# Steps of an mLSTM and of a second attention moved by a slab inside one TensorE-bound program

## The chip, the cores and the metric

One core of a Trainium2 chip runs the whole program. The metric is device microseconds of one execution (us). Three runs of the kernel before gave 877.93, 878.43 and 878.40 us, median 878.4.

## The reference, cut to what matters

Two transformer blocks run one after the other on 256 tokens of width 1024. The change touches only the middle of the second: its mLSTM branch (4 heads of 128), its attention branch (8 heads of 64) and the first product behind them.

```python
# second block, z = h @ w_in_2 split into mq, mk, mv, mo, mi, mf, aq, ak, av, ga, gb
hm = mlstm_chunkwise(q, k, v, i, f)      # W = exp(D - m), SW = (q k^T) * W, h = SW v / max(|sum SW|, exp(-m))
hm = rms_norm_2(hm, m_norm_g)            # over the 128 of each head
ym = hm * sigmoid(mo)
ya = merge_heads(moba_attention(rope(aq), rope(ak), av))     # softmax attention, causal
merged = sigmoid(ga) * (ym @ p_mlstm) + sigmoid(gb) * (ya @ p_moba)
x = x + g1 * (merged @ w_out)
```

## The kernel before

All weights are one stream of 298 **slabs**, each 128 x 1024 floats. SyncE loads slab n + 7 when slab n is worked (line 545, tile raw, five buffers). A slab is split into two parts: ScalarE copies it to whi (`high_part`, line 2048, four buffers), VectorE subtracts to get wlo (`low_part`, line 1146). TensorE makes three products of 128 x 128 by 256 for each of the 8 weight blocks of a slab (lines 1101, 1103, 1104 in this part), 24 for a slab.

Everything else is cut into **steps**: generators that yield after each step. The table `STEPS` gives for each task three lists, for TensorE, VectorE and ScalarE; a number n says that this engine takes the task's next step behind slab n of its own program (208.5 is the middle of slab 209). No planner looks at times: the order on every engine is what the lists say, each engine runs its queue in order, and semaphores make a step wait for its inputs. Steps with the same number run in the order of the dictionary: "mlstm" ahead of "att2" ahead of "gates2".

- TensorE at number n: the steps come behind the last product of slab n.
- ScalarE at n: first `high_part(n + 4)`, which waits until TensorE has finished slab n, then the steps.
- VectorE at n: first `low_part(n + 3)`, then the steps. For n equal to `LATE` the split comes behind the steps (lines 2023 to 2028). But where a pair of output tiles ends with slab n, `low_part(n + 3)` has already been called at the head of the pair's event, ahead of the steps of n: `low_part` does a slab once only. In the product "gab" (slabs 200 to 215) this holds for each odd n, 215 among them, and not for 214.

The steps of the two mLSTM halves (two heads each; TensorE / VectorE / ScalarE) are: gate rows to all partitions (833); weights' maxima (1612 to 1626) and exponentials (2274); q k products (842, 843); weighting (1636 to 1659); transposes (850) and their copy (2282); output products "h" (857, 859); squares (2286, 2291) with hb and nlo (1666, 1671); sum of squares "n" (865, 866); root (2295); reciprocals (1676), gain (1681) and gate (1687); high part Ymhi (2301); low part Ymlo (1604, function `low`). The attention has four pairs of heads, each: scores "s" (879, 880), maxima (1385 to 1395), exponentials (2159), weighting (1401, 1406), transposes "t" (887), copy (2169), outputs "o" (899, 901), high part (2191, 2193), low part (1429). The task "gates2" turns four gate tiles by a sigmoid (2308), twice at its step 213.

The product "pm" begins with slab 216. It takes heads 0 and 1 of Ymhi and Ymlo in the first half of each output pair, heads 2 and 3 in the second half, so in the second half of slab 216 TensorE waits for the mLSTM's last output.

Of the kernel before, what the change touches and what calls it, by code (L numbers as in the profile page):

```python
# [158 lines left out]
def slab_ends():  # L159

    out, u = {}, 0
    for name, (kind, w, lead, c0, m, K) in zip(NAMES, plan()):
# [5 lines left out]
        else:  # L168
            u += m // 128 * K
            if u % SLAB == 0:  # L170
# [13 lines left out]

ROPE = (0, 2, 1, 3)

LATE = 214

BETWEEN = {40: 3, 68: 7, 183: 5}
STEPS = {  # L190
# [19 lines left out]
    "final": ([], [199, 205, 211, 215], []),  # L210
    "ifg": ([186, 188], [182, 185, 187, 189], [182, 183, 188]),
    "rope": ([], [189, 192, 195, 197], []),
    "mlstm": ([191, 193, 195, 197, 199, 203, 206, 208.5, 209.5, 211],
# [6 lines left out]
    "mfin": ([], [173, 175, 177, 178], [174, 176, 178, 179]),  # L220
    "mconv": ([], [*range(179, 188), 188, 188, 189], [182, 185, 188, 190]),
# [57 lines left out]
def build(nc, A, out):  # L279
# [16 lines left out]
    with ctx:  # L296
# [832 lines left out]
        def vector_program(v):  # L1129
# [4 lines left out]
            def low_part(s):  # L1134
                if s >= NS or s in lows:
                    return
                lows.add(s)
                w.wait_ge(*hi.at(s))
                if s >= NHL:
                    w.wait_ge(*mm.at("slab", s - NHL))  # L1140
                if name := beside(s):
                    x, y = narrow(name, s, raw[:, s % NRAW, :], joined[name][0])
                    v.tensor_tensor(narrow(name, s, raw[:, s % NRAW, :], joined[name][1])[1], x, y.bitcast(F32),
                                    ALU.subtract).then_inc(*lo_v.up(s))
                    return
                v.tensor_tensor(wlo[:, s % NHL, :], raw[:, s % NRAW, :], whi[:, s % NHL, :].bitcast(F32),  # L1146
                                ALU.subtract).then_inc(*lo_v.up(s))
# [868 lines left out]
            for name in NAMES:  # L2016
                for what, n in EVENTS[name]:
                    if what == "pair":
# [3 lines left out]
                        continue  # L2022
                    if n == int(n) and n >= 1 and n != LATE:
                        low_part(int(n) + 3)
                    for task in v_steps.get(n, ()):
                        if task in tasks:
                            next(tasks[task], None)
                    if n == LATE:
                        low_part(int(n) + 3)
# [696 lines left out]
```

## Time and profile before

| | us |
|---|---|
| median of three runs | 878.4 |
| profiled execution, its own time | 878.33 |
| its span, first to last instruction | 877.0 |
| TensorE busy | 867.4 (99%) |
| VectorE busy | 725.4 (83%) |
| ScalarE busy | 573.4 (65%) |
| granted TensorE clock, mean | 0.998 |

Busy time adds up the instructions of an engine. Matmuls overlap in the pipeline, so 99% says that TensorE is nearly always in work and not that it runs at its peak. The 1.33 us between the execution's time and its span lie around the program.

### The profile page before, as it was taken

The numbers are of one execution on the slowest core, as the hardware profiler recorded it, in microseconds if no ns is written. First come the engines' busy times: TensorE is split into PE (matmuls) and PEld (weight loads), VectorE is DVE, ScalarE is ACT, GpSimd is POOL, SyncE is SP. The second block draws the span as 40 slices with busy tenths as digits, with TensorE's granted clock in tenths as the row PEclk, the third lists the DMA queues.
The fourth block names the chain that finished last, engine by engine and source line by source line (L and its number), as shares of the span: only waits on it lengthen the run. The fifth ranks groups of instructions, "written<-read, shape, count | busy, mean of one in ns | idle before, by whom it ended". The sixth has DMA issues, their size and how long they took to land.

```text
span 877.0 us, 18438 instructions
## 1 busy us (share of the span) xinstructions
PE 867.4 (99%) x7308; PEld 846.6 (97%) x7308; DVE 725.4 (83%) x1168; ACT 573.4 (65%) x851; POOL 2.2 (0%) x10
## 2 busy tenths in 40 slices
PE   9999999999999999999999999999999999999996
PEld 7999989999999999999999999899999999999996
DVE  6788999899988899888887999989788985555554
ACT  7858466675696787664446879677786664444542
POOL 0000000000000000000000000000000000000000
PEclk9999999999999999999999999999999999999999
DMA  8866456566775789989895566754455566666551
GB/s 316 284 197 225 149 164 194 170 191 211 271 243 191 257 290 332 324 299 339 328 336 180 168 220 209 209 166 141 152 166 176 187 201 200 192 194 195 182 161 49
DMA packets 59045, 189.87 MB, mean 216 GB/s; under 512 B 8640, under 2 KB 11088, under 8 KB 58832
## 3 DMA queue, kind: packets, MB, share of 16 engines
q1 hardware_dynamic: 58816, 188.69, 65.0%
q8 instruction: 59, 0.97, 0.5%
q14 instruction: 26, 0.21, 0.1%
q10 hardware_dynamic: 144, 0.00, 0.0%
HBM read 186.57 MB, written 1.05 MB: 214 GB/s over the span
## 4 chain that ended last, share of the span: by engine, by line
PE 91%; ACT 4%; DVE 3%; issue 1%; DMA 1%; SPq 0%; DVEq 0%; ACTq 0%
PE bank L1101 28%; PE bank L1103 27%; PE bank L1104 27%; PE bank L1074 1%; PE bank L1073 1%; PE bank L1072 1%; ACT whi L2048 1%; DMA H<-in_xT 1%; PE bank L1035 0%; DVE wlo L1146 0%; PE bank L1042 0%; PE bank L1038 0%; PE bank L887 0%; PE bank L769 0%; ACT L2252 0%
## 5 line engine op out<-in xcount | busy, mean ns | idle before, releaser
L1146 DVE TENSOR_TENSOR wlo<-raw,whi 128x1024 fp32r<-128x1024 f32 x291 | 353.7, 1221 | 83.2 <-ACT whi L2048 82.6
L2048 ACT ACTIVATE whi<-raw 128x1024 fp32r<-128x1024 f32 x291 | 304.7, 1056 | 169.0 <-PE bank L1104 164.2
L1101 PE MATMUL bank<-Alo,whi 128*128 128x256 f32 x1328 | 371.5, 280 | 0.0
L1103 PE MATMUL bank<-Ahi,wlo 128*128 128x256 f32 x1328 | 367.7, 277 | 0.0
L1104 PE MATMUL bank<-Ahi,whi 128*128 128x256 f32 x1328 | 367.7, 277 | 0.0
L1101 PEld LDWEIGHTS bank<-Alo,whi 128*128 128x128 f32 x1328 | 249.9, 188 | 2.8 <-issue 2.2
L1103 PEld LDWEIGHTS bank<-Ahi,wlo 128*128 128x128 f32 x1328 | 249.5, 188 | 0.4 <-issue 0.2
L1104 PEld LDWEIGHTS bank<-Ahi,whi 128*128 128x128 f32 x1328 | 249.5, 188 | 0.0
L1103 PE MATMUL bank<-Fhi,wlo 128*128 128x256 f32 (+1 forms) x320 | 88.9, 278 | 0.0
L1104 PE MATMUL bank<-Fhi,whi 128*128 128x256 f32 (+1 forms) x320 | 88.9, 278 | 0.0
L1101 PE MATMUL bank<-Flo,whi 128*128 128x256 f32 x256 | 70.8, 277 | 0.0
L1473 DVE SCALAR_TENSOR_TENSOR aacc<-arows,csil,aacc 128x768 f32<-128x768 f32 x63 | 63.8, 1013 | 0.0
L1103 PEld LDWEIGHTS bank<-Fhi,wlo 128*128 128x128 f32 x320 | 60.3, 188 | 0.0
L1104 PEld LDWEIGHTS bank<-Fhi,whi 128*128 128x128 f32 x320 | 60.3, 188 | 0.0
L1101 PE MATMUL bank<-Ylo,whi 128*128 128x256 f32 x192 | 53.7, 279 | 0.0
L1103 PE MATMUL bank<-Yhi,wlo 128*128 128x256 f32 x192 | 53.1, 276 | 0.0
L1104 PE MATMUL bank<-Yhi,whi 128*128 128x256 f32 x192 | 53.1, 276 | 0.0
L1245 DVE SCALAR_TENSOR_TENSOR cv<-ypad,cols,cv 128x256 f32<-128x256 f32 x120 | 51.5, 480 | 0.1
L1104 PE MATMUL bank<-Uhi,whi 128*128 128x256 f32 x176 | 48.6, 276 | 0.0
L1103 PE MATMUL bank<-Uhi,wlo 128*128 128x256 f32 x176 | 48.6, 276 | 0.0
L1101 PE MATMUL bank<-Ulo,whi 128*128 128x256 f32 x176 | 48.6, 276 | 0.0
L1101 PEld LDWEIGHTS bank<-Flo,whi 128*128 128x128 f32 x256 | 48.1, 188 | 0.0
(447 smaller groups left out, 1378.3 us busy)
## 6 DMA issues: line engine op xcount, KB each, us to landing
raw<-in_stream SPq DMA_DIRECT2D x298, 512.0 KB, 4.3
arows<-in_ada SPq DMA_DIRECT2D x64, 384.0 KB, 5.2
TB<-in_TB SPq DMA_DIRECT2D x1, 1536.0 KB, 7.2
a8r<-a SPq DMA_DIRECT2D x16, 64.0 KB, 4.2
out<-H SPq DMA_DIRECT2D x4, 256.0 KB, 2.9
bc<-in_bc SPq DMA_DIRECT2D x1, 896.0 KB, 5.7
H<-in_xT SPq DMA_DIRECT2D x1, 512.0 KB, 7.2
mats<-in_mats SPq DMA_DIRECT2D x1, 449.0 KB, 7.2
```

Source lines behind the costliest of these rows:

```text
L1072: pe.matmul(o, xl[:, ts], wh, start=k == 0, stop=False)
L1073: pe.matmul(o, xh[:, ts], wl, start=False, stop=False)
L1074: i = pe.matmul(o, xh[:, ts], wh, start=False, stop=last)
L1101: pe.matmul(os[j], wh, xl, start=k == 0 and (wide or j == 0), stop=False, skip_group_check=not wide)
L1103: pe.matmul(os[j], wl, xh, start=False, stop=False, skip_group_check=not wide)
L1104: i = pe.matmul(os[j], wh, xh, start=False, stop=k == K - 1 if wide else last, skip_group_check=not wide)
L1146: v.tensor_tensor(wlo[:, s % NHL, :], raw[:, s % NRAW, :], whi[:, s % NHL, :].bitcast(F32), ALU.subtract).then_inc(*lo_v.up(s))
L1245: v.scalar_tensor_tensor(out=o, in0=y, scalar=c, in1=o, op0=ALU.mult, op1=ALU.add).then_inc(*conv_v.up("tap", j, ct))
L1473: v.scalar_tensor_tensor(out=o, in0=arows[:, n % 4, :], scalar=c, in1=o, op0=ALU.mult, op1=ALU.add).then_inc(*ada_v.up(n))
L2048: a.activation(whi[:, s % NHL, :], raw[:, s % NRAW, :], ACT.Copy).then_inc(*hi.up(s))
```

## The change

Only numbers in tables change. Every instruction stays as it is; its place in its engine's order moves.

```diff
-LATE = 214
+LATE = 215
     "rope": ([], [189, 192, 195, 197], []),
-    "mlstm": ([191, 193, 195, 197, 199, 203, 206, 208.5, 209.5, 211],
-              [192, 194, 198, 201, 202, 204, 206, 207, 210, 213, 213, 214],
-              [192, 195, 197, 199, 205, 206, 208, 209, 211, 213]),
-    "att2": ([193, 198, 199, 199, 204, 205, 205, 210, 211, 211, 215.5, 217.5],
-             [194, 196, 200, 200, 201, 206, 206, 208, 212, 212, 213, 219],
-             [194, 198, 199, 200, 204, 205, 206, 210, 211, 212, 215, 218]),
+    "mlstm": ([191, 193, 195, 198, 200, 203, 206, 208.5, 210, 212],
+              [192, 194, 199, 202, 203, 204, 206, 207, 211, 213, 214, 215],
+              [192, 195, 198, 200, 205, 206, 208, 210, 212, 214]),
+    "att2": ([193, 198, 199, 199, 204, 206, 206, 210, 211, 211, 215.5, 217.5],
+             [194, 196, 200, 200, 201, 207, 207, 209, 212, 212, 213, 219],
+             [194, 198, 199, 200, 204, 206, 207, 210, 211, 212, 215, 218]),
```

On TensorE, "h" of the first half goes from 197 to 198 (beside "t" of the attention), its "n" from 199 to 200; "o" and "s" of the attention at 205 go to 206 (beside q k of the second half); "h" of the second half goes from 209.5 to 210 (beside "t"), its "n" from 211 to 212. On ScalarE and VectorE the steps that follow from these go a slab back; the first reciprocal of the second half stays at 213, the second with gain and gate goes to 214, Ymhi to 214 and Ymlo to 215.

## Rows read from the trace of the kernel before

**Rows 1.** The page, part 1: busy time, share of the span, instructions.
```profile
PE 867.4 (99%) x7308; PEld 846.6 (97%) x7308; DVE 725.4 (83%) x1168; ACT 573.4 (65%) x851; POOL 2.2 (0%) x10
```

**Rows 2.** Waits of TensorE, whole span: total, times, longest.
```profile
PE bank L1052 <- DVE ones L1989: 1.0, 1, 1.0
...
PE bank L857 <- ACT Wt L2282: 0.2, 1, 0.2
```

**Rows 3.** Timeline of TensorE around number 197: start, length, what, idle before.
```profile
577.64 0.28 PE L1104 MATMUL bank<-Ahi,whi 128*128 128x256 f32 x1
578.14 0.70 PE L857 MATMUL bank<-Wt,mv 128*128 128x256 f32 x2 [0.22 <-ACT Wt L2282]
```

**Rows 4.** Timeline of TensorE, behind "t" at 198, and "n" at 199.
```profile
582.95 0.37 PE L1101 MATMUL bank<-Alo,whi 128*128 128x256 f32 x1
583.15 0.28 PE L1103 MATMUL bank<-Ahi,wlo 128*128 128x256 f32 x1
...
585.78 0.28 PE L865 MATMUL bank<-nhi,onesr 128*128 128x256 f32 x1
...
586.34 0.44 PE L899 MATMUL bank<-P,av 128*64 128x256 f32 x2
```

**Rows 5.** Windows of 12 us, TensorE: length, busy (instructions), clock, DMA share, GB/s.
```profile
630.50:642.50 12.00, 12.00 (x103) 1.00 0.27 89
662.00:674.00 12.00, 12.00 (x108) 1.00 0.46 146
```

**Rows 6.** Timeline of TensorE: slab 213 begins, "t" at 215.5, head 2.
```profile
633.20 0.28 PE L1101 MATMUL bank<-Alo,whi 128*128 128x256 f32 x1
...
643.10 0.82 PE L887 MATMUL bank<-mats,P 128*128 128x128 f32 x6
643.67 0.37 PE L1101 MATMUL bank<-Ymlo,whi 128*128 128x256 f32 x1
```

**Rows 7.** Timeline of ScalarE, second half's root to the gates' sigmoids.
```profile
631.34 0.84 ACT L2295 ACTIVATE hsc<-bank,cols 128x256 f32<-128x256 f32 x2
...
633.46 1.06 ACT L2048 ACTIVATE whi<-raw 128x1024 fp32r<-128x1024 f32 x1 [0.47 <-PE bank L1104]
634.55 1.28 ACT L2159 ACT_TABLE_LOAD   x1
...
637.61 0.81 ACT L2364 ACTIVATE gab<-bank,cols 128x256 f32<-128x256 f32 x2
638.32 1.05 ACT L2048 ACTIVATE whi<-raw 128x1024 fp32r<-128x1024 f32 x1
641.10 0.76 ACT L2301 ACTIVATE Ymhi<-hsc 128x256 fp32r<-128x256 f32 x2 [1.73 <-DVE hsc L1687]
641.88 1.28 ACT L2308 ACT_TABLE_LOAD   x1
643.17 2.01 ACT L2308 ACTIVATE gab<-gab 128x1024 f32<-128x1024 f32 x2
645.09 1.04 ACT L2048 ACTIVATE whi<-raw 128x1024 fp32r<-128x1024 f32 x1
```

**Rows 8.** Timeline of VectorE in the same stretch.
```profile
636.68 3.36 DVE L1676 RECIPROCAL hsc<-hsc 128x256 f32<-128x256 f32 x2
...
640.65 0.76 DVE L1687 TENSOR_TENSOR hsc<-hsc,mo 128x256 f32<-128x256 f32 x2
...
642.44 0.75 DVE L1604 TENSOR_TENSOR Ymlo<-hsc,Ymhi 128x256 fp32r<-128x256 f32 x2
...
646.16 1.23 DVE L1146 TENSOR_TENSOR wlo<-raw,whi 128x1024 fp32r<-128x1024 f32 x1 [1.83 <-ACT whi L2048]
647.30 0.88 DVE L1539 SCALAR_TENSOR_TENSOR H<-H,cols,nrm 128x256 f32<-128x256 f32 x2
```

**Rows 9.** Timeline of ScalarE: the attention's third exponentials.
```profile
614.12 0.40 ACT L2159 ACTIVATE P<-P,stat 128x128 f32<-128x128 f32 x1 [0.83 <-DVE stat L1395]
```

**Rows 10.** Windows of 1 us at the program's end, columns as rows 5.
```profile
871.00:872.00 1.00, 0.46 (x3) 1.00 0.00 0
...
874.00:875.00 1.00, 0.00 (x0) 0.50 1.01 281
```

## The prediction

> **What bounds the kernel now.** I read the page's busy shares first: TensorE is in work for 867.4 of 877.0 us [rows 1]. Then its waits over the whole span: the longest is 1.0 us, before the first product, and in the stretch that changes there is one of 0.2 us, "h" of the first mLSTM half at number 197, for ScalarE's copy [rows 2]. So a moved step counts only by what it does to TensorE's own sequence, or by making TensorE wait. I took the timeline of TensorE for what its steps cost, and then those of ScalarE and VectorE between 630 and 648 us, where the mLSTM's last output is made just ahead of the product that takes it.
>
> There the margin is small. TensorE begins slab 213 at 633.20, the transposes at 215.5 run at 643.10, and the first product with head 2 starts at 643.67 [rows 6]. The low parts of heads 2 and 3 are one row of 0.75 us from 642.44 [rows 8]; head 2 is done about half of it later, at 642.85. The slack is 0.8 us, and a slab is 24 products, 2.7 us at the rate of 108 products in 12 us [rows 5].
>
> **What the change gives back on TensorE.** No instruction is added or removed. The moved steps issue no DMA and nothing passes a queue of SyncE or GpSimd; SyncE still loads a slab when the split of the slab five before it is done, and the DMA share in these stretches is 0.27 to 0.46 [rows 5], so I price those at zero; if a load were late it would show as ScalarE waiting for raw, and nothing here brings it nearer than the slabs it leads by.
>
> - "h" at 198 instead of 197: it starts 0.50 us behind the last product of its slab, with 0.22 us of idle for the copy [rows 3]. Products in the stream follow each other by about 0.11 us, so up to 0.38 us goes. The copy is then a slab old.
> - Two pairs now end in transposes ("h" with "t" at 198 and 210). After a group of steps the first stream product takes 0.20 us to the next instead of 0.11 [rows 4]; one return less is 0.09 each, 0.18 us for two. For the third pair (q k with "o" and "s" at 206) I see between 0 and 0.1 us and take 0, as the change from q k to "o" is a break of its own.
> - The stream has two rates. In one 12 us window 103 products fit, in another 108 [rows 5], at the same granted clock: 0.004 to 0.005 us per product. The slower rate stands behind "h" and behind "n" with "o" and "s", until the next group of transposes or gate rows; such stretches hold 240 products, 156 of them before slab 212's end. With "h" ahead of "t", 36 of these become fast, with "n" taken away from "o" and "s" 48 more, and behind a lone "n" (72 products) nothing in the trace tells. Between 0.35 and 0.7 us; I take 0.6.
> - "n" itself costs the same at 200 as at 199: four products, 585.78 to 586.34, less a break of 0.09, 0.47 us [rows 4]. But "n" of the second half leaves the work ahead of slab 212's end: 0.47 us earlier there, paid again at once behind it.
> - At 210 there is a price. The third scores now stand behind the weighting of the second half on VectorE, nearly a slab later, and ScalarE's exponentials at that point already waited 0.83 us for them [rows 9]; ScalarE's splits and the mLSTM's copy for "h" queue behind them. I count that "t" at 210 meets its input about 0.2 us late; bounds 0 and, if the whole scores' delay came through beyond the gained margin, 1.0 us.
>
> Sum at slab 212's end: 0.38 + 0.18 + 0.6 + 0.47 - 0.2 = 1.43 us earlier (0.9 to 1.8).
>
> **What it costs at slab 216.** Call E the end of slab 212, now 633.20 [rows 6]. Before, the second half's root ran at 631.34 [rows 7], ahead of E. Now "n" comes behind E, so root, exponentials, gates' sigmoids and Ymhi all stand in one queue of ScalarE behind E. Its length, from rows 7:
>
> split of 216 begins E + 0.26; to the table load 1.09; a table load 1.29; root of two heads 0.86; table load and exponentials 634.55 to 637.61, 3.06; copy of gab 0.71; split of 217 1.08; table load and two sigmoids 641.88 to 645.09, 3.21: the split of 218 begins at E + 11.56.
>
> Before, Ymhi stood ahead of the sigmoids (641.10 against 641.88), now it stands behind them and behind the split of 218. VectorE comes out level with this: the split of 217 begins at E + 7.27, its low part at 8.34 and ends at 9.48; the second reciprocal takes 1.65 (3.36 for two), gain 0.7 (636.68 to 640.65 less two reciprocals) and gate 0.7 [rows 8], so VectorE is through at E + 12.5. Before, both reciprocals, gain and gate ran as one block at 213; now the second stands behind the split of 217, which itself stands behind the exponentials.
>
> Then the order of VectorE: 215 ends an output pair, so the low part of slab 218 is called ahead of the steps of 215 whatever LATE says, where at 214 it was called behind them. It begins 1.07 us after its high part (645.09 to 646.16) and holds VectorE 1.14 us (to 647.30) [rows 7, 8]. Low part of head 2: 0.42, semaphore 0.05. Head 2 is ready at E + 11.56 + 1.07 + 1.14 + 0.47 = E + 14.24. Before, TensorE took it at 643.67, E + 10.47. So the point where head 2 starts moves by 14.24 - 10.47 - 1.43 = 2.3 us later, and TensorE, which is there at about E + 10.7 (0.47 for "n" added, 0.3 saved if the stream is fast), waits 3.5 us. Behind it no queue is short: whi and wlo of slabs 217 and 218 are done before TensorE asks for them, the gates are done, and both helper engines have slack again in the rest (VectorE was idle 1.83 us at 646 [rows 8]). The delay stays to the end.
>
> The profiled execution has 878.33 us for a span of 877.0, 0.1 below the median. 878.33 + 2.3 = 880.6 us.
>
> ScalarE's table loads are weighed here because three of them are in the queue. The row has 1.28 us, with the sigmoid starting at 643.17, 0.01 us after the load's end [rows 7]. The Trainium skill (ScalarE: Activation LUTs, section What ACT_TABLE_LOAD costs) gives 1.28 us and 1.38 us of drain beside it for each switch. By that figure the queue would be longer by three times 1.38; the trace does not show such a drain, and the sum goes by the rows.
>
> **The rivals.**
>
> 1. No wait of weight at pm (not slower): the outputs a slab back are still covered. It decides at the start of head 2: if Ymlo of head 2 ends before E + 10.7, TensorE keeps what it saved. Price: -1.43 + 0.47 + up to -0.4 for the 84 products behind slab 212 at the fast rate, about -1.1 us: 877.2 us, 876.3 to 877.8. For it: TensorE has not waited there so far. Against: a slack of 0.8 us for a move of one slab, and the sigmoids newly in front.
> 2. A shorter wait: the queue goes as I say but the low part of slab 218 does not come in between, or the sum of rows is long by as much: 1.14 us less, 879.5 us.
> 3. The wait also lowers the clock. In the last microseconds TensorE is in work for 0.46 of the window 871 to 872 at clock 1.00, and at 874 to 875 the granted clock is 0.50 (1.2 GHz), within 3 us of its last product [rows 10]. A wait of 3.5 us in mid-program has no like before. If it falls, each microsecond of stream at 1.2 GHz does half of one's work; how soon it comes back no row shows. Between 0 and the 2.7 us that two slabs at half rate would lose, I take 1.5: 882.1 us. The Trainium skill (TensorE: Matmul & The Clock Gate, Part 1) has the same two levels and halves the clock for an idle engine; it agrees with that row.
> 4. A second wait at 210: the third exponentials come a slab late and the copy for "h" with them; the whole delay counts, 1.0 instead of 0.2: 881.4 us.
> 5. The table loads drain as the skill says, visible where no work hides it: three times 1.38 (the page's figure) would be 884.7 us. In terms of rows, ScalarE would have a gap behind each load; the rows have 0.01 us.
>
> **How the numbers follow.** The forecast, 880.6 us with an own range of 879.9 to 881.6, gets 0.42; rival 1 0.20; rival 2 0.16; rival 3 0.14; rival 4 0.06; rival 5 0.02. A difference of 0.2% (1.8 us) is about what a measurement of this kernel tells from none: the bounds are 876.6 and 880.2. Faster: 0.08, all of rival 1. Within: 0.12 of rival 1, 0.15 of rival 2, 0.05 of the forecast, 0.32. Slower: 0.37 of the forecast, 0.14, 0.06, 0.02 and 0.01, 0.60. Range: 877.0 to 882.3 us; it leaves out nearly half of rival 1 below, and rival 5 and the worst of rival 3 above.
>
> **What would show it.** In the changed profile TensorE's waits have a new first row, the product with Ymlo waiting for VectorE, about 3.5 us (3 to 4); the 0.2 us of "h" is gone. ScalarE's timeline has the two sigmoids ahead of Ymhi, and VectorE's a weight split right ahead of Ymlo. Between "n" of the first half and 203 the count per 12 us is 103 or 108, which settles the lone "n". Up to the end of slab 212 the changed kernel is 1.4 us ahead, at the end 2.3 behind. The forecast is wrong if the wait is under 1 us, if Ymhi is done ahead of the sigmoids' end, or if the clock is below 1.00 near 646 us.

## The result, and the profile after

The changed kernel takes 884.04 us (median of 4, 883.6 to 885.18) against 878.41 for the kernel before: ratio 1.0064, 95% interval 1.0046 to 1.0081. It is slower by 5.6 us. The forecast was slower by 2.3 us, at 880.6, with a range up to 882.3; the direction and the place were right, the size was not.

The page of the changed kernel, part 1, answers to [rows 1]: its span is 882.2 us, 5.2 more than before. The counts of instructions are the same; TensorE's busy time is 1.8 us longer. The second fence is the list of TensorE's waits (total, times, longest), which answers to [rows 2].

```profile
PE 869.2 (99%) x7308; PEld 847.7 (96%) x7308; DVE 726.3 (82%) x1168; ACT 573.0 (65%) x851; POOL 2.2 (0%) x10
```

```profile
PE bank L1101 <- DVE Ymlo L1604: 3.9, 1, 3.9
PE bank L1052 <- DVE ones L1989: 1.0, 1, 1.0
```

The 0.2 us in front of "h" at 197 are gone from the list, and the product with Ymlo waits 3.9 us. TensorE's timeline at that place answers to [rows 6]:

```profile
642.48 0.82 PE L887 MATMUL bank<-mats,P 128*128 128x128 f32 x6
647.23 0.36 PE L1101 MATMUL bank<-Ymlo,whi 128*128 128x256 f32 x1 [3.93 <-DVE Ymlo L1604]
647.42 0.30 PE L1103 MATMUL bank<-Ymhi,wlo 128*128 128x256 f32 x1
...
648.17 0.41 PE L1104 MATMUL bank<-Ymhi,whi 128*128 128x256 f32 x1
648.38 0.41 PE L1101 MATMUL bank<-Ymlo,whi 128*128 128x256 f32 x1
```

Behind the wait the products start 0.21 us apart, where 0.11 is usual. The windows (length, busy and instructions, granted clock, DMA share, GB/s) say why: the granted clock is 1.00 up to 646 and falls as the stream comes back. It is 0.50, that is 1.2 GHz, at 648, and 1.00 again by 651.

```profile
644.00:646.00 2.00, 0.00 (x0) 1.00 0.29 117
646.00:648.00 2.00, 0.77 (x5) 0.89 0.51 127
648.00:649.00 1.00, 1.00 (x6) 0.50 0.65 262
...
651.00:652.00 1.00, 1.00 (x11) 1.00 0.42 168
```

ScalarE's timeline between slab 212's end (632.12) and Ymhi, to be read against [rows 7]: root, exponentials, gates' sigmoids and three splits of weights (slabs 216, 217 and 218) stand ahead of Ymhi without a gap.

```profile
632.38 1.06 ACT L2048 ACTIVATE whi<-raw 128x1024 fp32r<-128x1024 f32 x1 [2.06 <-PE bank L1104]
633.45 1.28 ACT L2295 ACT_TABLE_LOAD   x1
634.75 0.84 ACT L2295 ACTIVATE hsc<-bank,cols 128x256 f32<-128x256 f32 x2
635.61 1.28 ACT L2159 ACT_TABLE_LOAD   x1
...
638.67 0.81 ACT L2364 ACTIVATE gab<-bank,cols 128x256 f32<-128x256 f32 x2
639.38 1.05 ACT L2048 ACTIVATE whi<-raw 128x1024 fp32r<-128x1024 f32 x1
640.45 1.28 ACT L2308 ACT_TABLE_LOAD   x1
641.75 2.00 ACT L2308 ACTIVATE gab<-gab 128x1024 f32<-128x1024 f32 x2
643.66 1.04 ACT L2048 ACTIVATE whi<-raw 128x1024 fp32r<-128x1024 f32 x1
644.61 0.71 ACT L2301 ACTIVATE Ymhi<-hsc 128x256 fp32r<-128x256 f32 x2
```

VectorE in the same stretch, against [rows 8]. Between the gate product (L1687) and Ymlo stand the low part of slab 218 and a step of "final" (L1539), which the prediction had left out:

```profile
640.47 1.23 DVE L1146 TENSOR_TENSOR wlo<-raw,whi 128x1024 fp32r<-128x1024 f32 x1 [0.59 <-ACT whi L2048]
641.61 1.75 DVE L1676 RECIPROCAL hsc<-hsc 128x256 f32<-128x256 f32 x1
...
643.97 0.76 DVE L1687 TENSOR_TENSOR hsc<-hsc,mo 128x256 f32<-128x256 f32 x2
644.73 1.23 DVE L1146 TENSOR_TENSOR wlo<-raw,whi 128x1024 fp32r<-128x1024 f32 x1
645.87 0.88 DVE L1539 SCALAR_TENSOR_TENSOR H<-H,cols,nrm 128x256 f32<-128x256 f32 x2
646.66 0.75 DVE L1604 TENSOR_TENSOR Ymlo<-hsc,Ymhi 128x256 fp32r<-128x256 f32 x2
```

**Where the 5.6 us are.** The profiled executions differ by up to 1.2 us ahead of the change (571.08 to 572.25 in the table), so I measure each kernel from a point that the change does not reach: the mLSTM's transposes at 195 (L850, first). The first stage ends where head 2 starts, the second at the sum of squares behind wo2 (L652).

| kernel | transposes at 195 | head 2 starts | L652 | stage 1 | stage 2 | wait at Ymlo |
|---|---|---|---|---|---|---|
| before | 571.57 | 643.67 | 691.68 | 72.10 | 48.01 | none |
| changed | 571.08 | 647.23 | 696.84 | 76.15 | 49.61 | 3.9 |
| e1 tail back | 571.32 | 643.21 | 691.20 | 71.89 | 47.99 | none |
| e2 busy wait | 571.46 | 647.73 | 695.73 | 76.27 | 48.00 | 0.8 and the extras |
| e3 split behind | 571.77 | 646.91 | 697.77 | 75.14 | 50.86 | 2.7 |
| e4 both behind | 571.95 | 646.45 | 694.63 | 74.50 | 48.18 | 2.3 |
| e5 and gates | 571.22 | 645.49 | 695.09 | 74.27 | 49.60 | 2.1 |
| e6 tail alone | 571.47 | 645.58 | 693.59 | 74.11 | 48.01 | 2.3 |
| e7 first, middle | 572.06 | 645.12 | 693.13 | 73.06 | 48.01 | none |
| e8 plain | 571.61 | 643.80 | 691.81 | 72.19 | 48.01 | none |
| e9 first, third | 572.25 | 645.05 | 693.05 | 72.80 | 48.00 | none |

The change adds 4.05 us in stage 1 and 1.60 in stage 2, 5.65 together; the medians differ by 5.63. Each stage is read from one execution. Stage 1 is good to about 0.4 us: the products between 572 and 580, which the same steps surround in both, start 0.1136 us apart in the changed kernel and 0.1177 in e2 (71 products, 0.3 us), and 95 products from 588 on take 0.4 us less in e6 than in the kernel before. A smaller difference of stage 1 tells nothing by itself.

### The profile page after: what moved, and what is told of

It reads as the page before. It is cut to its first block, busy times and chain, and to the rows that moved or that the text cites. A ratio compares the mean times of both kernels' runs of the same rounds, so it can differ in the third digit from the quotient of the medians.

```text
span 882.2 us, 18438 instructions
## 1 busy us (share of the span) xinstructions
PE 869.2 (99%) x7308; PEld 847.7 (96%) x7308; DVE 726.3 (82%) x1168; ACT 573.0 (65%) x851; POOL 2.2 (0%) x10
## 4 chain that ended last, share of the span: by engine, by line
PE 91%; ACT 4%; DVE 3%; issue 1%; DMA 0%; SPq 0%; DVEq 0%; ACTq 0%
PE bank L1101 27%; PE bank L1104 27%; PE bank L1103 27%; PE bank L1072 1%; PE bank L1074 1%; PE bank L1073 1%; ACT whi L2048 1%; DVE wlo L1146 1%; PE bank L1035 1%; DMA raw<-in_stream 0%; PE bank L1042 0%; PE bank L1038 0%; DVE mqk L1567 0%; PE bank L769 0%; DVE t L1188 0%
```

## The experiments

e1 to e4 and e9 ran on one chip, e5 to e8 on another, each batch with new runs of the kernel before on the same chip; their medians are 878.4 to 878.6 us. Each ratio is to these.

### e1: the outputs' last steps back at their places

The changed kernel with

```diff
-LATE = 215
+LATE = 214
-              [192, 194, 199, 202, 203, 204, 206, 207, 211, 213, 214, 215],
-              [192, 195, 198, 200, 205, 206, 208, 210, 212, 214]),
+              [192, 194, 199, 202, 203, 204, 206, 207, 211, 213, 213, 214],
+              [192, 195, 198, 200, 205, 206, 208, 210, 212, 213]),
```

> The changed kernel with the mLSTM's last steps at their old places: both reciprocals, gain and gate of the second half at 213 on VectorE, Ymhi at 213 and Ymlo at 214, LATE 214. All TensorE numbers stay those of the change, n of the second half at 212 included. Theory (the wait at pm and what it brings make the loss): Ymhi is done ahead of the sigmoids, near 641 us, Ymlo near 642, before TensorE is at head 2 (about 643.1); the wait of 3.9 us is gone, the clock stays at 1.00, and the time is 877.5 to 878.3 us, level with before or a little under it. Rival (the moved TensorE steps cost the time themselves, in breaks and in the stream's slow rate): 882 to 884 us, with no wait.

Measured: 878.54 us (10 runs), ratio to before 1.0003 (0.9994 to 1.0013). The wait is gone; TensorE goes from the transposes at 215.5 straight to head 2, and VectorE begins the low part at 641.17. First fence TensorE, second VectorE:

```profile
642.63 0.82 PE L887 MATMUL bank<-mats,P 128*128 128x128 f32 x6
643.21 0.37 PE L1101 MATMUL bank<-Ymlo,whi 128*128 128x256 f32 x1
```

```profile
641.17 0.75 DVE L1604 TENSOR_TENSOR Ymlo<-hsc,Ymhi 128x256 fp32r<-128x256 f32 x2
```

With four numbers at the tail put back, all of the loss is gone: the moved TensorE steps, the later "n" among them, cost nothing by themselves. (With the moved tail they do cost; see e6.) The time is 0.2 us above the expected range. Stage 1 went from 72.10 to 71.89 us, which is within what one execution can tell, so no gain from the moves on TensorE is shown either.

### e2: TensorE kept busy through the wait

```diff
                         i.then_inc(*att2_pe.up("t", hp, hf))
+                    if hp == 3:
+                        w.wait_ge(*ml_s.at("root", 1, 0))
+                        for _ in range(14):
+                            plain(3)
                     yield
```

> The changed kernel with 14 extra products into a free PSUM bank behind the transposes at 215.5, so that TensorE works through most of its wait (3.4 of 3.9 us). They add nothing to the result. Theory (1.6 us of the loss are the granted clock's fall after the idle wait): the clock stays at 1.00 and the time is 1.6 us under the changed kernel, 882.2 to 882.7 us, head 2 starting at the same time as there. Rival (the slow products behind the wait are starved by late splits or memory, not by the clock): 884 us, products behind the wait again 0.21 us apart.

Measured: 882.92 us (4 runs), ratio 1.0051 (1.0036 to 1.0066). The clock stays at 1.00 and stage 2 is 48.00 us, as before the change; stage 1 is as in the changed kernel (76.27). The windows:

```profile
644.00:646.00 2.00, 2.00 (x21) 1.00 0.51 205
646.00:650.00 4.00, 3.19 (x29) 1.00 0.37 131
```

So extra work that computes nothing makes the kernel faster by 1.1 us in the median (all four executions are below all four of the changed kernel), and stage 2 by 1.6: the slow products behind the wait were the clock, and no split or load was late. The median fell by less than the 1.3 to 1.8 expected; head 2 starts 0.1 later here, the rest is within what 4 runs tell.

### e3 and e4: VectorE's queue ahead of Ymlo

e3 keeps the low part of 218 behind the steps of 215; e4 moves the step of "final" as well.

```diff
-                        if (name, n) in ENDS and ENDS[name, n] >= 1 and name != "pg" and (name, n) not in (("br3", 3), ("pa", 3)):
+                        if (name, n) in ENDS and ENDS[name, n] >= 1 and name != "pg" and (name, n) not in (("br3", 3), ("pa", 3), ("gab", 7)):
```

e4 has besides:

```diff
-    "final": ([], [199, 205, 211, 215], []),
+    "final": ([], [199, 205, 211, 216], []),
```

> The changed kernel, but VectorE makes the low part of slab 218 behind the steps of 215 instead of at the head of the pair's event. Theory (VectorE's queue ahead of Ymlo sets the wait: split 1.14, final 0.79): Ymlo 1.1 us earlier, the wait at pm 2.8 instead of 3.9 us; the time 1.1 us less if the clock still falls (883 us), 2.7 less if it does not (881.3). Rival (ScalarE's queue of table loads and sigmoids alone sets it): Ymlo moves by less than 0.4 us, 883.7 to 884.

> As the run with the split behind, and the last step of final (0.79 us on VectorE) at 216 instead of 215. Theory: Ymlo directly behind Ymhi, near 645.1; the wait 2.1 to 2.3 us; 1.7 us under the changed kernel with a fall of the clock, 3.3 under it without (880.7). Rival: as above, no more than 0.4 us.

Measured: e3 883.51 us (4 runs, 881.4 to 884.69), ratio 1.0055 (1.004 to 1.007); e4 882.16 us (881.41 to 882.9), ratio 1.0042 (1.0027 to 1.0057). The waits follow the theory: 1.2 us shorter than in the changed kernel in e3, 1.6 in e4 (stage 1: 1.0 and 1.65 shorter). Waits, e3 and e4:

```profile
PE bank L1101 <- DVE Ymlo L1604: 2.7, 1, 2.7
```

```profile
PE bank L1101 <- DVE Ymlo L1604: 2.3, 1, 2.3
```

The times do not follow the waits one for one, because of the clock. In e3's profiled execution it is down for longer than in the changed kernel, in e4's it does not fall at all. Windows of e3, then of e4:

```profile
646.00:650.00 4.00, 3.09 (x14) 0.53 0.20 31
650.00:654.00 4.00, 4.00 (x25) 0.62 0.83 245
```

```profile
646.00:650.00 4.00, 3.55 (x30) 1.00 0.27 80
650.00:654.00 4.00, 4.00 (x36) 1.00 0.85 244
```

Stage 2 is 50.86 us in e3, 2.85 more than in the kernel before, with a shorter wait than the changed kernel's. The other executions have no trace, only a mean clock. Among e4's four executions two have a mean clock of 0.997 and take 881.41 and 881.42 us, two have 0.994 and 0.995 and take 882.9. e3 has 881.4 at 0.997, 883.2 at 0.994, 883.8 at 0.995 and 884.7 at 0.993. If the differences are the clock's, as the means suggest, e4 loses nothing or 1.5 us to it, and e3 nothing, 1.8, 2.4 or 3.3.

### e5: the sigmoids behind Ymhi

On top of e4:

```diff
-    "gates2": ([], [], [213, 218]),
+    "gates2": ([], [], [214, 218]),
```

> The changed kernel with VectorE's two steps out of the way as in the run before (low part of 218 and final behind Ymlo), and the two sigmoids of the gates at 214, behind Ymhi. It asks which queue sets the wait once VectorE's two are gone. In the run with both behind, Ymlo waited 0.31 us for Ymhi, and Ymhi for the sigmoids. Theory (two queues of nearly one length lead to the same point, so each alone hides the other): Ymhi now waits for the gate product, near 645.2, Ymlo starts 0.3 us earlier or less than that; the wait is 1.9 to 2.3 us; 880.5 to 882 us. Rival (the sigmoids' 3.2 us were the cause): the wait falls by 2 us or more, to under 0.5 us, and the time to 879 us or less.

Measured: 881.83 us (6 runs), ratio 1.0039 (1.0027 to 1.0052); the wait is 2.1 us, 0.2 us shorter than in e4, and so is stage 1. The granted clock falls in the profiled execution (stage 2 is 49.60 us). With its 3.2 us of table load and sigmoids out of the way ScalarE stands idle and waits for VectorE:

```profile
644.47 0.75 ACT L2301 ACTIVATE Ymhi<-hsc 128x256 fp32r<-128x256 f32 x2 [3.04 <-DVE hsc L1687]
```

The two queues were of nearly one length: once VectorE's two steps are gone (e4), Ymlo waits 0.31 us for ScalarE's Ymhi, and once the sigmoids are gone too, Ymhi waits for VectorE. What the wait of 2.1 us that is left comes from was read from timelines and not tried by itself. In VectorE's queue it is the second reciprocal, which stands behind the split of 217, which stands behind the exponentials on ScalarE: it starts at 641.66 here, and the gate product at 644.02, where in e1, with both reciprocals in one block, the gate product starts at 639.39.

### e6: the tail alone

The kernel before with the numbers that e1 took away, TensorE's and the root's (211) untouched.

```diff
-LATE = 214
+LATE = 215
-              [192, 194, 198, 201, 202, 204, 206, 207, 210, 213, 213, 214],
-              [192, 195, 197, 199, 205, 206, 208, 209, 211, 213]),
+              [192, 194, 198, 201, 202, 204, 206, 207, 210, 213, 214, 215],
+              [192, 195, 197, 199, 205, 206, 208, 209, 211, 214]),
```

> The kernel before with only the end of the mLSTM moved: second reciprocal, gain and gate at 214, Ymhi at 214, Ymlo at 215, LATE 215; TensorE's numbers and the root's (211) as before. Theory (the order in the helpers' queues costs most of it, n at 212 only some of it): head 2 waits for Ymlo, which comes at about 646.0 behind the split of 218 and final; the wait is 2.3 to 2.7 us; 881 to 882 us, up to 883.5 in executions whose clock falls. Rival (the wait comes from n and root behind slab 212): the wait is under 1 us, 878.5 to 879.2 us.

Measured: 881.88 us (5 runs), ratio 1.0037 (1.0024 to 1.005), a wait of 2.3 us, stage 1 2.0 us longer than before. Of the 4.05 us of stage 1, half is the order of the tail by itself. The other half comes only with both: the moved TensorE steps with the old tail cost nothing (e1), the tail alone 2.0, together 4.05. With "n" at 212 the root comes behind the end of slab 212 and not ahead of it. In e1 Ymlo starts at 641.17 all the same, 2.0 us ahead of head 2. Behind the moved tail nothing is left to cover the delay: VectorE ends the gate product 10.5 us behind the end of slab 212 in e6 and 12.6 us behind it in the changed kernel.

### e7 and e9: two pairs of the three

Both are the kernel before with the "mlstm" or "att2" numbers of the change for two of the pairs, and the outputs' ends as before. e7 has the first half (h 198, n 200) and the middle (o, s at 206), with h at 209.5 and n at 211. e9 has the first half and the second (h 210, n 212), with the attention as before.

> The kernel before with two of the three pairs: the first half's h and n at 198 and 200 with what follows, and the attention's o and s at 206 with what follows. The second half's h, n and outputs stay as before. Theory: 0.58 us from the first pair (the wait of 0.4 and two breaks), nothing from the middle one, and no late transposes at 210 since h stands alone; 877.8 to 878.2 us. Rival (late third scores cost at 209.5 as they did at 210, 0.4 us): 878.3 to 878.8 us with TensorE waiting at h or t there.

> The kernel before with the first and the third pair of the mLSTM (h at 198 and 210, n at 200 and 212, with what follows) and the outputs' ends at their old places (VectorE 213, 213, 214, ScalarE 213, LATE 214); the attention's steps all as before, so its third scores are not late. Theory: the wait of the first h is gone (0.4), h and t share two breaks (0.2), neither h, t nor the product with Ymlo waits; 877.4 to 878.1 us, 0.5 to 1.1 under before. Rival (what TensorE gives up at one place it waits for at the next, since VectorE and ScalarE keep their pace in this stretch): a new wait of 0.3 us or more at the transposes of 208.5 or at h, and 878.2 to 878.8 us, level with before.

Measured: e7 879.75 us (10 runs), ratio 1.0014 (1.0005 to 1.0023); e9 879.37 us (11 runs), ratio 1.0012 (1.0003 to 1.0021). Both rivals held in kind (TensorE waits at "h" in e7 and at the transposes in e9), and the times are 0.6 to 1 us above even theirs: two pairs are slower than none and slower than three (e1). TensorE's waits there, e7's in the first fence (the list of waits) and e9's in the second (its timeline, transposes of the second half):

```profile
PE bank L857 <- ACT Wt L2282: 1.3, 1, 1.3
```

```profile
619.76 0.55 PE L850 MATMUL bank<-mats,Wp 128*128 128x128 f32 x3 [0.76 <-DVE Wp L1659]
```

In e7 the third scores stand behind the weighting, ScalarE's exponentials wait 3.7 us for them, the copy for "h" stands behind these, and at 209.5 TensorE meets it 1.3 us early. In e9 the first half's reciprocals, moved by a slab, stand later in VectorE's queue, the scores stay ahead of the weighting, and TensorE is at the transposes of 208.5 0.8 us early. As I read it, the middle pair lets VectorE weight first and the third pair gives "h" the time for its late copy: the three belong together, and end level with where they began. This is argued from the timelines; the middle with the third pair, and each pair alone, were not run.

### e8: an extra product behind each lone "n"

```diff
                                   ).then_inc(*ml_pe.up("n", hp, i))
+                    w.wait_ge(*att2_s.at("o", 2 * hp))
+                    plain(7)
                     yield
```

> The run with the tail back, with one extra product of 128 columns (0.25 us, into a free bank) behind each lone n, at 200 and 212. Stream products behind the lone n were 0.117 us apart. Theory (the slow rate is a state that the kind of product ahead of the stream sets): behind the extra product they are 0.113 apart in both stretches, 156 products by 0.004, 0.6 us, against 0.5 us for the two extras. Rival (the rate is set by what the other engines do there): 0.117 in both stretches still.

Measured: one execution of 878.44 us; stage 1 0.30 us longer than e1. Counts of TensorE's instructions in the windows 591 to 598 and 634 to 641, e8:

```profile
591.00:598.00 7.00, 7.00 (x62) 1.00 0.36 114
634.00:641.00 7.00, 7.00 (x62) 1.00 0.25 83
```

and in e6, where TensorE's order is that of the kernel before:

```profile
591.00:598.00 7.00, 7.00 (x64) 1.00 0.33 110
```

The kernel before has 61 in the first of these windows. A count takes in the products that lie across the window's ends, so 61 and 62 both stand for 0.118 us a product and 64 for 0.1135, as their starts in the timeline have it. So the extra product does not bring the fast rate, and the same order of instructions runs at 0.118 in one execution and at 0.1135 in another. The theory that the kind of the last step sets the rate falls; what does set it stays open.

## Why the prediction failed in size

The mechanism of the forecast, a wait at head 2 behind a longer queue, came as described. Three steps failed: the queue ahead of Ymlo left out one step of VectorE (0.87 us too short), the gain set against it was 0.84 us too large, and the clock's fall, 1.60 us, was kept as a rival and put at nothing in the sum. The clock is the largest of the three; no one of them alone takes the time beyond the range. In the prediction's own terms:

- **The queue at slab 216**: forecast 14.24 us from the end of slab 212 to head 2, measured 632.12 to 647.23, 15.11 us. The terms of ScalarE are right to 0.02: the split of 218 begins 11.54 us behind the slab's end, forecast 11.56. Missing is the step of "final" at 215, 0.79 us on VectorE, which the dictionary puts ahead of "mlstm" (645.87 to 646.66 above; without it, in e4 against e3, the wait is 0.4 us shorter, and Ymhi is then what Ymlo waits for). I had read the order of mlstm, att2 and gates2 at one number and not of all names there.
- **The low part of slab 218 at the head of the pair's event**, whatever LATE says: right, 1.14 us; e3 takes just it away, and the wait is 1.2 us shorter. LATE 215 does not do what it seems to.
- **Two queues of one length**: right to 0.3 us (e4 and e5).
- **Earlier by 1.43 us at the end of slab 212**: measured 0.59: from the transposes at 195 to that point 633.20 - 571.57 = 61.63 us before, 632.12 - 571.08 = 61.04 after. The wait at 197 and the first break came (0.58 up to 203), and so did the 0.47 of "n". The slow rate did not go: products are 0.118 apart behind the lone "n", at 200 and at 212, and behind "t" at 198, so most of the 0.6 is missing. That term tied the rate to the kind of step from a single execution; the runs show both rates behind the same steps. Its size was read from counts, 12 us over 103 and over 108, which differ by 0.0054 and not by 0.004 to 0.005; by the products' starts it is 0.004. And at 210 the sum had 0.11 us of loss (0.2 late, less a break of 0.09), where 0.48 were lost: from the transposes at 208.5 to the first product behind "t" 6.69 us before (618.53 to 625.22), 7.17 after (617.43 to 624.60). "h" starts at 622.29, 0.1 us later than it could, and "t" at 623.84 lasts 1.01 us, where a free one takes 0.82.
- **The clock**: rival 3, to which I gave 0.14. It was the case in all four runs of the changed kernel (means 0.993 to 0.995, against 0.996 to 0.998 for the kernel before). I took 1.5 us for it; the profile has 1.60. The rows at the program's end [rows 10] had shown the fall, within 3 us of the last product, less than the 3.5 us of wait that I forecast; the weight that I gave it did not follow from that row.

Forecast 880.6; with 0.87 for the queue, 0.84 for the missing gain and 1.60 for the clock it is 883.9, measured 884.04. That the sum meets the median to 0.1 us is partly luck, since its terms are read from one execution of each kernel. Rival 1 (no wait) fell with the first row of the waits; rival 2 with e3, since the split does come in between; rival 4 was right in kind at 210, but "h" and "t" are together 0.4 us late there and not 1.0 (in e7, where "h" stands half a slab earlier, the wait is 1.3 us). Rival 5 fell: ScalarE's next instruction starts 0.01 to 0.02 us behind the end of each of the three table loads of 1.28 us (633.45 to 634.75, 635.61 to 636.90, 640.45 to 641.75). The Trainium skill (ScalarE: Activation LUTs, What ACT_TABLE_LOAD costs) gives 1.28 us for a load and 1.38 us of drain beside it. The load agrees with these rows; the drain does not show in them.

## What to carry to other kernels

When a step is moved by one place in a queue written by hand, list the whole queue between its last input and its user on every engine, with all tasks at that number, and compare the sum with the slack; a slab of 2.8 us cannot be hidden in 0.8 us of slack. Where the bounding engine is made to wait amid dense work, put the price of the clock beside the wait: here waits of 2.1 to 3.9 us cost from nothing to 2.85 us more behind them. When one queue is shortened and nothing moves, look for a second one of the same length before the first is acquitted.

## What the hardware showed unexpectedly

A single wait of TensorE in the midst of dense work can cost up to about its own length again behind it. In the changed kernel (wait 3.9 us) the granted clock fell from 1.00 to 0.50 about when the stream came back and was back at 1.00 at 651 (1.6 us lost); in e3 (2.7 us) it was at 0.50 until 653 (2.85 us lost). The length of the wait does not decide it alone: in the profiled executions it fell behind 2.1 us in e5 and stayed at 1.00 behind 2.3 us in e4 and e6. A window just behind the wait, e5 and then e6:

```profile
646.00:647.00 1.00, 1.00 (x7) 0.50 0.00 0
```

```profile
646.00:647.00 1.00, 1.00 (x11) 1.00 0.86 336
```

By their mean clocks it fell in some executions of e3, e4 and e6 and not in others. That TensorE's clock is at half behind idle time is what the Trainium skill says (TensorE: Matmul & The Clock Gate, Part 1). The changed kernel, e3 and e5 agree, and e2 agrees from the other side: products into a bank that nobody reads held it at 1.00.

The stream of 128 x 128 by 256 products has two rates at the full clock, 0.1135 and 0.118 us. In these traces either one lasts until the next group of other steps. They are not tied to the order of the instructions (e6 against the kernel before, e2 against the changed kernel); neither the kernel's other engines nor the last step's kind was shown to set them.
